# Starting the attention of a hybrid decoder layer with a middle block, and moving one transpose and one gate unit on TensorE

## The reference

```python
hn = _rms_norm(h, norm_gain)
(c_q, c_kv, k_idx, w_idx, z_attn, q_g, k_g, v_g, z_g, b_g, a_g) = _split_last(hn @ w_in, IN_PROJ_SPLITS)
# group A: 8 heads x 64, top-256 causal keys per query chosen by a token indexer
idx_score = jnp.einsum('bqh,bqhs->bqs', wb, jax.nn.relu(idx_logits))
_, sel = lax.top_k(idx_score, topk)
p = jax.nn.softmax(where(valid, q . k[sel] * scale + bias, -inf))
o_attn = (p @ v[sel]) * jax.nn.silu(z_attn)
# group B: 4 heads x 128, gated DeltaNet: conv, silu, chunked WY form, a state S carried from chunk to chunk
v_new = u_i - w_i @ S
o = qd_i @ S + aqk_i @ v_new
S = S * cd_i + kd_i^T @ v_new
o_gdn = _rms_norm(o, g_out) * jax.nn.silu(z_g)
y = concat([o_attn, o_gdn]) @ w_out
return h + y
```

## Time and profile before

| what | value |
| --- | --- |
| median of 3 runs | 862.48 us (859.11 to 863.02) |
| profiled execution | 861.26 us |
| its span in the profile | 859.5 us |
| mean granted TensorE clock | 0.98 of full |
| TensorE busy | 813.5 us, 95% |
| VectorE busy | 606.4 us, 71% |
| ScalarE busy | 388.4 us, 45% |
| GpSimd busy | 251.8 us, 29% |

### The profile page before, as it was taken

The page is one execution under the profiler, slowest core; times in us unless marked ns, Lnnn a source line. Parts: engine busy times, 40 slices in busy tenths (PEclk is TensorE's granted clock), DMA queues, the critical chain, the costliest instruction groups (busy, mean ns, idle before and its releaser), DMA issues.

```text
span 859.5 us, 16494 instructions
## 1 busy us (share of the span) xinstructions
PE 813.5 (95%) x6345; PEld 488.3 (57%) x6345; DVE 606.4 (71%) x1405; ACT 388.4 (45%) x1218; POOL 251.8 (29%) x254
## 2 busy tenths in 40 slices
PE   6999999999999999999969999999899999999998
PEld 2554434444446666666625677766676566566564
DVE  2344689999999999999766567667656565575541
ACT  3443656777792555555434445575322122022111
POOL 8000000000000636476642532355232332233210
PEclk9999999999999999999979999999879999999999
DMA  6252200030003001000100200203320220222011
GB/s 174 70 210 98 75 23 27 24 124 37 25 14 123 1 23 75 1 1 0 50 25 1 99 26 28 88 25 121 116 97 30 99 99 25 76 76 75 26 51 50
DMA packets 29507, 51.72 MB, mean 60 GB/s; under 512 B 3684, under 2 KB 11220, under 8 KB 29428
## 3 DMA queue, kind: packets, MB, share of 16 engines
q1 hardware_dynamic: 28884, 50.55, 17.4%
q0 software_dynamic: 544, 0.10, 0.3%
HBM read 40.11 MB, written 12.10 MB: 61 GB/s over the span
## 4 chain that ended last, share of the span: by engine, by line
PE 86%; DVE 6%; ACT 4%; issue 3%; DMA 1%; POOL 0%; DVEq 0%; ACTq 0%; POOLq 0%
PE ps L1682 20%; PE ps L1893 12%; PE ps L1660 11%; PE ps L1537 7%; PE ps L1731 5%; PE ps L1720 5%; PE ps L1702 4%; PE ps L1794 2%; PE ps L1634 2%; PE ps L1814 1%; PE ps L1588 1%; PE ps L1855 1%; PE ps L1830 1%; PE ps L1847 1%; PE ps L1869 1%
## 5 line engine op out<-in xcount | busy, mean ns | idle before, releaser
L1199 DVE TENSOR_SCALAR_CACHE_REDUCE junk<-scores,iw 128x272 bf16<-128x272 f32 (+6 forms) x224 | 213.6, 954 | 8.2
L1682 PE MATMUL ps<-areaH,areaW 128*128 128x384 f32 (+1 forms) x576 | 168.1, 455 | 1.6 <-ACT areaQ L935 1.6
L1682 PEld LDWEIGHTS ps<-areaH,areaW 128*128 128x128 f32 x576 | 109.4, 190 | 59.8 <-issue 1.8
L747 POOL TENSOR_TENSOR staging<-staging,areaC 128x520 f32<-128x520 f32 x60 | 88.0, 1504 | 63.9 <-ACT areaC L973 63.9
L761 POOL TENSOR_TENSOR areaH<-areaQ,masks 128x512 f32<-128x512 f32 x37 | 45.3, 1229 | 91.3 <-PE ps L1814 83.5
L794 POOL TENSOR_TENSOR areaW<-scores,tmp 128x256 f32<-128x256 f32 (+1 forms) x64 | 44.9, 726 | 61.4 <-DVE small L1285 52.0
L1537 PE MATMUL ps<-areaW,areaH 128*128 128x460 f32 (+1 forms) x144 | 59.5, 568 | 1.9 <-DVE areaH L1121 1.9
L1893 PE MATMUL ps<-areaW,scores 128*128 128x512 f32 x128 | 59.2, 604 | 0.0
L973 ACT ACTIVATE areaC<-areaC,small 128x520 f32<-128x520 f32 x60 | 42.5, 724 | 34.0 <-POOL staging L747 34.0
L1660 PE MATMUL ps<-areaH,areaW 128*128 128x512 f32 x128 | 56.3, 594 | 0.0
L1660 PE MATMUL ps<-areaW,areaH 128*128 128x512 f32 x128 | 56.2, 592 | 0.0
(11 more groups left out here) (272 smaller groups left out, 1439.9 us busy)
## 6 DMA issues: line engine op xcount, KB each, us to landing
areaW<-in_w_in SPq DMA_DIRECT2D x5, 2048.0 KB, 8.1
areaH<-row_factor_scratch SPq DMA_DIRECT2D x18, 256.0 KB, 4.3
areaC<-in_x SPq DMA_DIRECT2D x8, 512.0 KB, 3.5
tmp<-in_x SPq DMA_DIRECT2D x8, 512.0 KB, 4.8
y<-tmp SPq DMA_DIRECT2D x7, 512.0 KB, 3.3
areaW<-in_w_out SPq DMA_DIRECT2D x3, 768.0 KB, 5.7
gate_a_scratch<-staging SPq DMA_DIRECT2D x8, 256.0 KB, 2.3
gate_g_scratch<-staging SPq DMA_DIRECT2D x8, 256.0 KB, 2.0
```

Source lines behind the costliest of these rows:

```text
L747: nc.gpsimd.tensor_tensor(sums, sums, prod, ALU.add).then_inc(s_cvP, 1)
L1199: tlink(V.tensor_scalar(junk[:, 0:n], scores[:, SC0[i]:SC0[i] + n], at, init, op, ALU.add, accum_out=cnt[:, i - 1:i]))
L1682: ins = mm(ps[:, n % 4, 0:hi - lo], wslot[:, g % 2, k, 128 * m:128 * m + 128], hT[:, k, lo:hi], start=k == 0, stop=k == KD - 1)
```

## The change

Three edits, and two numbers that follow from the second.

```diff
-REC_AT = [(["v"], []), ([], ["os"]), (["p0"], []), (["g", "p1"], []), (["yt", "p2"], ["ks"]), (["c", "p3"], []),
+REC_AT = [(["v"], []), ([], ["os"]), (["p0"], []), (["g", "p1"], []), (["p2"], ["yt", "ks"]), (["c", "p3"], []),
...
-        BLOCK = list(reversed(range(NB)))
+        BLOCK = [4, 7, 6, 5, 3, 2, 1, 0]
+        FULL = HP * BLOCK.index(NB - 1)
...
-                if st == 0:
+                if st == FULL:
                     now += [("meta", 0, "D"), ("meta", 1, "D")]
...
-        GATES = [(2 * t, 2 * t + 1) for t in range(6)] + [(12,), (13,), (14,), (15,)]
+        GATES = [(0,)] + [(2 * t - 1, 2 * t) for t in range(1, 7)] + [(13,), (14,), (15,)]
...
                 sp.dma_start(zA[:, i % 2, :], za_d[BLOCK[i]].rearrange("p m t -> p (m t)")).then_inc(s_za[i % 2], 16)
-                if i == 2:
+                if i == 3:
                     load_out(0, 5, 8)
                     load_out(1, 5, 8)
...
-                if step == 0:
+                if step == FULL:
                     read_ring("meta", 0)
                     read_ring("meta", 1)
```

## The result

| kernel | median (us) | runs |
| --- | --- | --- |
| before | 860.8 (858.66 to 863.02) | 4 |
| after | 847.49 (845.98 to 850.14) | 4 |

The ratio is 0.9853, with a 95% interval of 0.9824 to 0.9882: the change takes off 13.3 us by the medians and between 10.2 and 15.1 by the interval. The forecast was 850.5 with a range of 845 to 857. The profiled execution of after took 850.14 us, span 848.4, mean granted clock 0.982, the lowest clock of its four runs. Against the profiled execution of before (861.26) that is 11.1 us, where the sum had said 11.3.

A forecast was written before the change was run, and what follows sets the result against it. TensorE, holding 86% of the chain, was taken as the bound, through idle and low-clock time. Gains of 1.6 + 5.0 + 4.7 = 11.3 us off 861.26 gave 850.0; the forecast was put at 850.5, range 845 to 857.

The forecast's parts named there:

- the sum: Whole kernel: the gains from gate units, transpose and block order added to 11.3 us off the profiled 861.26.
- The gate units: Phase 2: slot 0 gives its second unit to slot 6, so the wait ahead of `up(7)` goes; gain 1.6 us.
- The slack of 1.0 us in slot 0: Phase 2, slot 0: ScalarE finishes at 118.5, one unit keeps TensorE busy until 119.5, so no wait, 1.0 us spare.
- The transposes: Phase 5: `yt` behind `x2` saves 0.93 us per tile, 5.0 us in all; 0.45 of each wait passes to `x2`.
- Rival B: Phase 5: the transpose's wait only changes its name, since VectorE is busy without a break; 854.7 us, 8%.
- The order of the blocks: Attention's first steps: beginning with block 4 loses less to idling and low clock; gain 4.7 us, bounds 1.3 and 7.0.
- the ring: Block 7's steps: TensorE waits for ring entries, 0.35 us in step 5, 1.1 in step 6, 1.7 lost altogether.
- The step by step picture: Attention's first pairs, worked out one by one: some 19 us from first logits to meta logits, low clock under 10 us.
- Rival A: Attention's first steps: clock stays at 1.2 GHz until block 7, or the ring costs as much; 853.4 us, 17%.
- Rival C: First attention steps and phase 5: the clock doesn't fall and `x2` waits less; 845.5 us, 8%.
- Rivals D and E: D: clock low through block 7's four steps, about 880 us, 3%. E: no change that can be told, 4%.
- D's first step: Block 7's steps: VectorE's 3.4 us leave gaps in TensorE's work and the clock stays low; about 880 us, 3%.

The follow-up runs named there:

- e1: Kernel before with only the gate units redistributed; median 854.89 us, ratio 0.995.
- e3: Kernel before with only the block order changed, with the meta tile and two loads that follow from it; median 854.29 us, ratio 0.9943.
- e2: Kernel before with only the transpose `yt` moved behind `p2` and `x2`; median 854.41 us, ratio 0.9949.
- e5: Changed kernel beginning with block 5 in place of block 4; median 849.2 us, ratio 0.9883 against before.
- e7: Changed kernel with VectorE's gated output behind the younger tile's preparatory operations; median 848.28 us, ratio 0.9874 against before.
- e10: Changed kernel with VectorE's gated output behind the younger tile's operations and `yt` behind `ks` on TensorE; median 843.11 us, ratio 0.9815 against before.
- e9: Changed kernel with unread filler products, 4 ahead of pair 1's logits and 2 ahead of pair 2's; median 844.99 us, ratio 0.9829 against before.
- e8: Changed kernel with the sums of squares started at step 8 in place of 4; median 853.27 us, ratio 0.9936 against before.
- e11: Changed kernel with the edits of e9 and e10 together; median 842.35 us, ratio 0.9816 against before.
- e4: Changed kernel with unread filler products, 8 ahead of pair 1's logits and 4 ahead of pair 2's; median 851.12 us, ratio 0.9909 against before.

## Why the prediction was right, point by point

- **The gate units.** Predicted 1.6, measured 1.8 (e1: 1.87). The slack of 1.0 us in slot 0 was real: nothing waits at 120.08. The attention began earlier by the same amount, so VectorE's threshold search did not stand in the way.
- **The transposes.** Predicted 0.93 per tile, measured 0.95 (31.03 to 30.08). VectorE's run from the output to the block is as long as before (667.14 to 669.13, 1.99 us, as in the earlier trace rows), and it starts as long behind the start of `x32` (1.35 us behind 665.79; in before 1.34 behind 671.63). `x2` idles 0.63 us and not 0.45 for two small reasons: `p2` starts 0.16 us ahead of the end that the profile gives for `x32`, where the sum had it start at that end, and `x2` follows the block by 0.14 us and not 0.06. Counted from `x32`, `x2` comes 1.34 us earlier (predicted 1.43) and `yt` costs 0.49, which makes 0.85; the last 0.10 of the period stands in `ks`, whose row takes 1.06 us in place of 1.16. Over the whole of phase 5 the term is 5.2 to 5.3 in three pairs of profiles with like time at the low clock (before and after 5.26, e3 and e2 5.23, e1 and e5 5.20), so the 5.0 does not hang on one execution. Rival B is excluded: the wait changed its name for 0.63 of the 1.38 us only, and e7 and e10 show that even that part is an order of readiness on VectorE and not work.
- **The order of the blocks.** Predicted 4.7, measured 4.55, and here terms were mis-sized with opposite signs. Block 7's logits take 1.92 us at full clock (456.60 to 458.52), where I took 1.75 from a row that already belongs to a smaller block's shape; so before had lost 14.8 and not 15.5. In return the ring costs 0.84 in step 6 and 0.28 in step 5 (its twelve transposes take 1.74 us, 461.45 to 463.19, where those of step 4 take 1.46), together 1.1 where I had 1.7. Up to the start of block 7 it is 20.3 us (430.41 to about 450.7) against the 20.0 worked out, 9.4 lost against 9.1: 14.8 - 9.4 - 1.1 = 4.3, and the remaining 0.25 I cannot place. Of the 4.55 the waits are 2.5: 3.92, 3.31 and one of 2.25 behind them for a ring copy before, 4.20, 1.99 and 0.84 now. The other 2.0 are rows that no longer run at the low clock. That 4.55 comes so near to 4.7 is luck in part. Over all profiles with either order and no other edit there, before's order takes 177.72 to 179.32 us and the new one 174.54 to 175.69, so the gain lies between 2.0 and 4.8, 3.6 by the means (178.6 and 175.0). Against e1, whose clock was back early, the whole gain is shorter waits (10.3 us in e1's first steps, 7.0 in after). The prediction's reading that the clock of before fell behind both long waits was not quite right either: it fell once, at 439.9 us, was still low when the second wait came, and fell again behind the third, of 2.25 us.
- **The step by step picture** of the first pairs held: 19.0 us from the first logits to the first meta logits (predicted some 19), transposes 2.11 at 443.02, full clock from the logits of pair 3. The low clock lasted 10.2 us where the prediction said under 10. Pair 1's logits were at the low clock throughout (2.56), which the prediction had left between 1.3 and 2.8.
- **Rival A** needed the clock to stay low until block 7. It came back within the run without gaps from 440.53 on, some 6 us ahead of block 7. The Trainium skill (TensorE: Matmul & The Clock Gate, HAM oscillation) says that bursts between waits start cold and that a stretch without gaps is the remedy. The trace agrees with both halves in these steps: the two bursts behind the gaps of 4.20 and 1.99 us took 2.56 where 1.38 is the full-clock time, and e9, whose gaps are 0.5 us, has no low clock there. Elsewhere long waits are not needed for it: after is at 1.2 GHz from 611.5 to 628.6 us, in phase 5, and no wait of TensorE there or in the ten microseconds ahead is over 0.9 us. Only its case against this edit did not hold, since the edit shortens the second gap and lengthens the run behind it.
- **Rival C** (845.5) was wrong in the profile on both counts, yet the median lies only 2 us above it. The medians moved 2.2 us more than the profiled executions, since after's profiled run was the slowest of its four, 2.7 above its median, and before's only 0.5 above; the sum, made against one profiled execution, had no term for the clock that differs from run to run. So the median lies 3.0 us under the forecast, further than the three terms are off together, and still inside the range.
- **Rivals D and E** did not occur. e8 shows D's first step at the price of 4.5 us.

## What to carry to other kernels

Begin a pipelined phase with a work item that the slow engine reads quickly, and count time at the lower clock as part of the price of a fill: here up to 2.0 of the 4.55 us that the new order gained was rows that take less time, not waits, and how much it is changed from profile to profile. A transpose or another short piece that waits for a second engine belongs behind everything that is ready without it, and behind it once more if the wait reappears on its neighbour: two such moves, the second with VectorE's output moved too, were worth 0.95 and 0.65 us per tile. Work that looks like a burden beside a slow engine may be its cover, so it is to be moved only after looking at what waits next.

## What the runs showed of the hardware

- The time follows the mean granted clock by 0.6 us per 0.001, within runs of one kernel. In phase 5, 10.3 us more at 1.2 GHz go with 3.7 us more time (e10 against e11, 236.29 and 239.97 with 6.8 and 17.1 us low; e5 against after the same 3.7, e1 against before 3.8), less than the 5.2 that half a clock's work would be.
- Eight records of 64x512 took 3.59 us on the filler of e9, which uses rows 0 to 63 alone, and eight records of the logits, which alternate between the two halves of the rows, 1.99 us in after. The logits' records start in pairs 0.01 us apart, one of each half, and the filler's one by one, 0.43 apart. Whether that is the rows or the one PSUM bank that all of the filler writes, no run separates.
- The length of a wait does not tell by itself whether the clock falls behind it. It fell behind 2.25 us in before (at 453.5), 1.89 in e2 (454.2) and 2.97 in e8 (471.9), and stayed full behind 3.13 in e1.
- A few thrown-away products in a gap hold the clock: with gaps of 4.20 and 1.99 us it was at 1.2 GHz for 10.2 us, with the filler of e9 for none, and the phase was 2.73 us shorter. The filler of e4, which does not fit into the gaps, held it too and made the phase 1.6 us longer.
- A 16-column operation on VectorE took 1.61 us while a GpSimd operation ran, and 0.17 us when none did (e8); it ended 0.03 us behind the GpSimd operation. The Trainium skill (SBUF — State Buffer, SBUF: two separate sides) says that a VectorE operation with two SBUF inputs and a GpSimd operation that reads SBUF take turns whole, the later one blocked until the other ends. This row agrees: both its inputs are in SBUF, and so is the GpSimd operation's. It is the only such meeting of this VectorE line in e8, and the ends are not exact: by the profile the operation's last 0.14 us lie ahead of the other's end.
